# Query absorption of attention heads 1 to 15 as three passes over rounded and remainder operands

## What is computed

```python
def _mla_queries(q_dn, q_norm, w_uq, w_uk):
    q = (_rmsnorm(q_dn, q_norm) @ w_uq).reshape(b, n, MLA_HEADS, MLA_NOPE + MLA_ROPE)
    q_abs = jnp.einsum('bnhd,chd->bnhc', q[..., :MLA_NOPE], w_uk)
    return q_abs, q[..., MLA_NOPE:]
# then: softmax(q_abs . c + q_rope . k_rope), p @ c, times w_uv, gated
```

## Time and profile before

| | |
|---|---|
| runs shown | 2151.46, 2155.03, 2546.47 us; median 2155.03 us |
| the profiled execution's own time | 2159.1 us |
| its span, first to last instruction | 2157.3 us |
| TensorE busy, whole span | 2040.7 us (95%) |
| VectorE, ScalarE, GpSimd busy | 1291.7 (60%), 837.6 (39%), 455.1 (21%) us |
| mean granted TensorE clock | 0.976 of full |
| TensorE's share of the chain that ended last | 85% |
| abs products of all 16 heads, L2580 | 128 records, first start 642.2, last 1047.4 us |

### The profile page before, as it was taken

One profiled execution on the slowest core, in us unless ns is written; L12 is line 12 of the kernel. 1 busy time (PEld: TensorE's weight loads), 2 busy tenths in 40 slices (PEclk: granted clock), 3 DMA queues, 4 the chain that ended last, 5 costly groups with the idle time before them and its releaser, 6 DMA issues.

```text
span 2157.3 us, 39613 instructions
## 1 busy us (share of the span) xinstructions
PE 2040.7 (95%) x16166; PEld 1550.2 (72%) x16166; DVE 1291.7 (60%) x1932; ACT 837.6 (39%) x1504; POOL 455.1 (21%) x400
## 2 busy tenths in 40 slices
PE   7999998899998999999899979999989999999997
PEld 6787787778885565555556547888867788888785
DVE  3356565468966677666558766888973233333344
ACT  3325443343314444444434046555534323232223
POOL 2543121230019996000001211111120000000000
PEclk9999899999999999999999989999999999999998
DMA  9231343432451121111279726999964233333321
GB/s 366 81 90 58 121 158 136 146 132 93 160 188 66 64 88 74 40 42 42 82 271 362 264 76 192 305 303 301 307 195 156 87 99 98 94 94 96 97 88 40
DMA packets 124597, 310.36 MB, mean 144 GB/s; under 512 B 12048, under 2 KB 58000, under 8 KB 118016
## 3 DMA queue, kind: packets, MB, share of 16 engines
q1 hardware_dynamic: 109952, 238.95, 34.0%
q0 software_dynamic: 9856, 49.99, 6.2%
q10 hardware_dynamic: 4608, 18.88, 2.3%
HBM read 233.45 MB, written 74.32 MB: 143 GB/s over the span
## 4 chain that ended last, share of the span: by engine, by line
PE 85%; DVE 7%; issue 4%; ACT 3%; POOL 0%; DMA 0%; SPq 0%; ACTq 0%; DVEq 0%; POOLq 0%
PE psum L517 30%; PE psum L2792 8%; PE psum L1988 7%; PE psum L2969 6%; PE psum L2543 5%; PE psum L2506 3%; PE psum L1189 3%; PE psum L2518 3%; PE psum L2593 2%; PE psum L3139 2%; PE psum L330 2%; PE psum L3089 1%; PE psum L3198 1%; PE psum L2532 1%; PE psum L2550 1%
## 5 line engine op out<-in xcount | busy, mean ns | idle before, releaser
L517 PE MATMUL psum<-split,w_split 128*128 128x512 f32 x1632 | 371.7, 389 | 0.0
L517 PEld LDWEIGHTS psum<-split,w_split 128*128 128x128 f32 x1632 | 306.3, 188 | 64.0 <-DVE w_split L499 0.4
L499 DVE TENSOR_TENSOR w_split<-ring,w_split 128x512 fp32r<-128x512 f32 x182 | 129.0, 709 | 309.7 <-ACT w_split L494 309.3
L494 ACT ACTIVATE w_split<-ring 128x512 fp32r<-128x512 f32 x182 | 115.0, 632 | 336.7 <-PE psum L517 333.7
L2792 PE MATMUL psum<-gate,ring 128*128 128x512 f32 (+1 forms) x512 | 165.4, 486 | 1.2 <-issue 1.2
L2969 PE MATMUL psum<-h,u_w 128*128 128x256 f32 (+1 forms) x768 | 157.4, 350 | 7.8 <-DVE h L2899 5.7
L2792 PEld LDWEIGHTS psum<-gate,ring 128*128 128x128 f32 x512 | 97.2, 190 | 69.3 <-issue 62.7
L517 PE MATMUL psum<-h,w_split 128*128 128x512 f32 x552 | 134.7, 404 | 7.9 <-DVE w_split L499 7.9
L517 PE MATMUL psum<-h_split,in_w 128*128 128x512 f32 x600 | 139.0, 391 | 1.5 <-POOL in_w L506 1.5
L2969 PEld LDWEIGHTS psum<-h,u_w 128*128 128x128 f32 x768 | 118.6, 191 | 27.2 <-issue 11.8
L517 PEld LDWEIGHTS psum<-h,w_split 128*128 128x128 f32 x552 | 106.4, 194 | 34.9 <-DVE w_split L499 5.4
(11 more groups left out here) (467 smaller groups left out, 3976.6 us busy)
## 6 DMA issues: line engine op xcount, KB each, us to landing
ring<-in_s_glu SPq DMA_DIRECT2D x64, 512.0 KB, 3.6
ring<-in_w_mod SPq DMA_DIRECT2D x48, 512.0 KB, 5.5
c_pow<-made_c_pow SPq DMA_DIRECT2D x32, 576.0 KB, 5.2
ring<-in_s_in SPq DMA_DIRECT2D x32, 512.0 KB, 6.5
made_b_pow<-area POOLq DMA_DIRECT2D x15, 1024.0 KB, 6.4
b_pow<-made_b_pow SPq DMA_DIRECT2D x15, 1024.0 KB, 10.6
ring<-in_w_in SPq DMA_DIRECT2D x25, 512.0 KB, 3.7
made_table<-table_made ACTq DMA_DIRECT2D x16, 768.0 KB, 5.7
```

Of the source, the lines that this page charges most:

```text
L494: nc.scalar.activation(rounded(buffer(u, 0)), source(u), ACT.Copy).then_inc(act_done, 1)
L499: nc.vector.tensor_tensor(rounded(buffer(u, 1)), source(u), buffer(u, 0), ALU.subtract).then_inc(dve_done, 1)
L517: ins = nc.tensor.matmul(out, rounded(buffer(u, w)[:, ks]), values(x, k), start=(first and k == 0 and n == 0), stop=(last and k == UNIT_K ...
```

## The change

For heads 1 to 15 the abs step is made of three passes over operands rounded to float32r (high) and their remainders (low): high times high, high times low, low times high. Head 0 stays in full float32, since it is made before head 0's own loop.

The rounded operands have to be made. `qn` is split once, in head 0: ScalarE rounds all 1536 columns (`qn_high_act`), between the exponentials of unit 2 and the copies of unit 0; VectorE subtracts (`qn_low_dve`, two instructions of 768 columns) at the end of head 0's middle pair. The folded weights are split in each head: ScalarE rounds 256 columns right after the copy to `folded`; VectorE subtracts (`head_rests_dve`, 256 columns) at the end of the middle pair, ahead of the gating and of the maxima of units 4 and 5. The abs step waits for these. The new tiles lie in room that is free at that time, so no buffer moves.

```diff
@@ head_pe, project
                 if what == "abs":
                     pe.wait_ge(*at("folded", hh))
+                    if hh >= 1:
+                        pe.wait_ge(*at("folded_low", hh))
+                        pe.wait_ge(*at("qn_low", 1))
...
                     for o, a, n in parts_of(0):
-                        for k in range(2):
-                            ins = mm(o, folded[:, k, :], qn[:, k, a:a + n], start=(k == 0), stop=(k == 1))
+                        if hh == 0:
+                            for k in range(2):
+                                ins = mm(o, folded[:, k, :], qn[:, k, a:a + n], start=(k == 0), stop=(k == 1))
+                        else:
+                            for k in range(2):
+                                for left, right in ((folded_high(hh), qn_high), (folded_high(hh), qn_low), (folded_low, qn_high)):
+                                    ins = mm(o, rounded(left[:, k, :]), rounded(right[k][:, a:a + n]) if right is qn_low else
+                                             rounded(right[:, k, a:a + n]),
+                                             start=(k == 0 and left is not folded_low and right is qn_high),
+                                             stop=(k == 1 and left is folded_low))
...
+        def qn_high_act(act):
+            act.wait_ge(*at("qn"))
+            act.wait_ge(*at("mla_in", "mm", 19))
+            nc.scalar.activation(rounded(qn_high), qn[:, :, :], ACT.Copy).then_inc(act_done, 1)
+            act_count.up("qn_high")
+
+        def qn_low_dve(dve):
+
+            dve.wait_ge(*at("qn_high"))
+            for k in range(2):
+                nc.vector.tensor_tensor(rounded(qn_low[k]), qn[:, k, :], qn_high[:, k, :], ALU.subtract).then_inc(dve_done, 1)
+                dve_count.up("qn_low", k)
+
+        def head_rests_dve(dve, h):
+
+            if h >= HEADS:
+                return
+            dve.wait_ge(*at("folded_high", h))
+            nc.vector.tensor_tensor(rounded(folded_low), folded[:, :, :], folded_high(h), ALU.subtract).then_inc(dve_done, 1)
+            dve_count.up("folded_low", h)
...
@@ proj_act
                 act.wait_ge(act_done, act_count.up("folded", h))
+                if h >= 1:
+                    nc.scalar.activation(rounded(folded_high(h)), folded[:, :, :], ACT.Copy).then_inc(act_done, 1)
+                    act_count.up("folded_high", h)
...
@@ head_act
             exp_act(act, n + 2)
+            if h == 0:
+                qn_high_act(act)
             pt_act(act, n)
...
@@ head_dve
                 normalize_dve(dve, n + 2 * pair + 1)
+                if pair == 1:
+                    head_rests_dve(dve, h + 1)
+                if pair == 1 and h == 0:
+                    qn_low_dve(dve)
```

More of the change, by code:

```diff
@@ L1808, in build @@
         at_early = ExitStack()
-        h2_low = sb(at_early, "h2_low", [KD, TC])
+        early_split = sb(at_early, "early_split", [KE * T])
         at_early.close()
@@ L1848, in build @@
         h2 = early_part(0, KD * TC).rearrange("p (k t) -> p k t", k=KD)
+        h2_low = early_split[:, 0:KD * TC].rearrange("p (k t) -> p k t", k=KD)
         q_raw = early_part(KD * TC, 2 * TC).rearrange("p (k t) -> p k t", k=2)
@@ L1851, in build @@
         folded = early_part(B_SPLIT, 2 * P).rearrange("p (k c) -> p k c", k=2)
+        qn_high = early_split[:, 2400:2400 + 2 * TC].rearrange("p (k t) -> p k t", k=2)
+        qn_low = [early_split[:, 4352:4352 + TC], ctx_high[:, :, :].rearrange("p k t -> p (k t)")[:, N_C_POW // 2:N_C_POW // 2 + TC]]
+        folded_low = early_split[:, B_SPLIT:B_SPLIT + 2 * P].rearrange("p (k c) -> p k c", k=2)
         sm = early_part(B_SPLIT + 2 * P, 12).rearrange("p (k c) -> p k c", k=3)
@@ L2627, in head_pe, with folded_high @@
             project(h + 1, "rope")
+        def folded_high(h):
+            return slot_split(("head", h))[:, 768:1024].rearrange("p (k c) -> p k c", k=2)
+        def qn_high_act(act):
[14 more added lines that the diff above has]
+            dve_count.up("folded_low", h)
         def softmax_dve(dve, n):
```

## The result

The changed kernel takes 2163.12 us (median of 17 runs, 2158.54 to 2172.71) against 2157.59 us before (17 runs); the ratio of the two is 1.0039, interval 1.0027 to 1.0052. The two medians are 5.5 us apart, but the kernel before has two slow executions among its 17 (2284.71 and 2546.47 us), which the ratio leaves out. By the ratio the loss is 8.4 us, with 5.8 to 11.2 us as its interval, and I go by ratios throughout. Within 2% it counts as no change, but it is a loss clear of noise, and more than twice the 2.5 us that was forecast even at the lower end.

What follows compares the result with a forecast made beforehand. TensorE is busiest, but a parallel chain through ScalarE and VectorE was taken to set rope's start and cover abs. Terms: heads 0, head 0 +2.5 us; 2155.0 + 2.5 = 2157.5 us, own range 2154 to 2162, wide range 2149 to 2165.

Steps and rivals of the forecast that it cites:

- Abs is covered; the saving is worth nothing on the path: Abs in each head falls from 2.58 to 2.18 us, but a ScalarE and VectorE chain sets rope's start: 0.
- Rival A: Abs's gain reaches the end: 15 x 0.40 = 6.0 us off, head 0's 2.5 us stay, 2151.5 us; chance 0.17.
- The folded weights' rounding and remainder cost nothing: Done 15 times: rounding about 0.38 us on ScalarE, remainder 0.49 us on VectorE, both fitting into idle time; cost 0.
- the 2.45 us of room: VectorE idle time behind unit 3's division, 1.51 + 0.53 + 0.41 us, that the weights' remainder can take before a head lengthens.
- Head 0: 2.5 us: The query's one-time split in head 0 makes rope of head 1 late by 1.8 to 3.1 us; 2.5 taken.
- ScalarE part: Rounding the query's 1536 columns in head 0 takes about 1.5 us, uncovered, and delays unit 5's scores by 1.5 us.
- VectorE part: Head 0's query and weights' remainders, 2.4 us, end 0.7 to 2.0 us later than the scores are ready.
- rival B: VectorE contention beside GpSimd, 1 us in seven heads, plus 7 us with clock drop in head 0: +14, 2169 us; chance 0.16.
- the upper end, 7 us: Head 0's cost if both parts of the query's remainder are held as long as the 2.42 us row.
- Heads 1 to 14: 0: No change from these heads: period still 26.6 us, waits ahead of abs fulfilled when TensorE gets there.
- the wide range, 2149 to 2165 us: Range of the total time taking in rival A wholly and half of rival B.

Runs made afterwards that it cites:

- One pass: Changed kernel with two of abs's three passes left out, high times high only; ratio to the kernel before 1.0081.
- six passes: Changed kernel with abs's three passes made twice over; ratio to the kernel before 1.0108.
- the two moves on the chain: VectorE's absorbed-query remainder before unit 4's division, ScalarE's context-column rounding before its exponential: kernel before 0.9979; changed kernel, query split before head 0's loop, 0.9951.
- GpSimd later: GpSimd's tables held back until after head 7; ratio to the kernel before 0.9991 on the changed kernel, 0.9981 on the kernel before.
- splits only with GpSimd later: Changed kernel with split work kept, abs of heads 1 to 15 as four float32 products, GpSimd's tables begun after head 7; 0.9982 to the kernel before.

## Why the prediction was right and wrong

- *Abs is covered; the saving is worth nothing on the path.* Right. Abs 2.19 us (forecast 2.18), period unchanged, wait ahead of rope 0.69 us (forecast about 0.6). One pass, six passes and the two moves on the chain show it from three sides. Rival A is out.
- *The folded weights' rounding and remainder cost nothing.* Right in quiet heads. Beside GpSimd the remainder took up to 2.64 us, and once, in head 6, 2.26 us behind a division that was late itself (1.40 us): the 2.45 us of room had been counted from an undisturbed head. Of the 2.5 us that head 6 is longer, this is at most 0.8; 1.7 us are rope at 4.50 us instead of 2.80, behind a wait of 2.42 us at the end of head 5, where the division on the chain took 2.07 us. Taken out of contention the remainder did not move the time measurably.
- *Head 0: 2.5 us.* This is the term that failed. By itself its ScalarE part is right: rounding 1.49 us, TensorE idle 1.42 us, 1.36 us in all where nothing else disturbed it. Its VectorE part, 1 us for remainders that hold back unit 4's maximum, was not there: the maximum waited for TensorE (0.40 us). What the sum left out is 2.8 us of TensorE at half pace behind the new idle time, which I had as part of rival B only, although show such a spell in this very head, and about 2 us of a stretched division (2.57 us) on the now late chain. With the 1.4 us of idle time these make 6.1 of the 6.2 us that head 0 lost in the profile. I took the upper end, 7 us, for unlikely. That head 0 without GpSimd beside it is 2.8 us longer, near the forecast's 2.5, is luck: half of it is again the lower clock.
- *Heads 1 to 14: 0.* They lost 3.1 us in the profile: heads 5 and 6 together 4.1 us, by a division of 2.07 us on the chain, the slow rope behind it and the late remainder, while heads 1 and 7 gave back 1.2. This is rival B's contention, and the runs with GpSimd later show whose it is.
- *Rival B* had the right mechanism (contention on VectorE with a clock drop in head 0) and the wrong spread: 14 us, with 1 us in each of seven heads. It came as two heads of about +2 us, one or two shorter ones, and the rest in head 0. The Trainium skill's rule on two-source instructions (SBUF — State Buffer, the section on the two separate sides) fits the weights' remainder, 0.42 us alone and up to 2.64 us beside GpSimd, but what lengthened heads were divisions, and with the remainder out of the way the time stayed.
- *The size.* 2163.12 us lies inside the wide range, 2149 to 2165 us, and past the forecast's own, which ended at 2162 us.

## What to carry over

A small idle time that the same instruction ends in every round can mark a parallel chain: measure it from its common start, before pricing anything that it runs beside; here the saving counted only once the chain was shorter. Work that is done once belongs where the engines are idle anyway, and its price is not its duration but what the stall sets off, the clock of TensorE included.

## Not expected

- Idle time alone did not tell whether TensorE's pace would fall. After 2.23 us rope took 2.80 us before (head 1); after 1.42 us unit 5's scores ran at half pace in the changed kernel; after 1.44 us at the same place they ran at pace in splits only with GpSimd later. I can't say from these runs what decides.
- GpSimd beside heads 8 to 15 lengthened no head by more than 0.2 us. Taking it away from heads 0 to 7 was worth about 4 us in the kernel before (0.9981) and 10 in the changed one (1.0039 to 0.9991).
